# Sixteen gate tiles of the input projection, moved from the scan stage into the prompt attention

## What is computed

```python
h = rmsnorm(x, g_mix)
z = h @ w_in                    # 2048 x 8192: q | k | v | u | gate_a | gate_s
gate_a = sigmoid(z[..., U_END:U_END + D_MODEL])       # 16 column tiles of 128
gate_s = sigmoid(z[..., U_END + D_MODEL:])            # 16 column tiles of 128
q, k = partial_rope(rmsnorm(q, g_q), pos), partial_rope(rmsnorm(k, g_k), pos)
att = diff_attention(q, pos, segments, lam)   # (softmax1 - lam * softmax2) @ v, 8 heads, causal
branch_a = rmsnorm(att, g_head) * (1 - lam_init) @ w_attn_up
branch_s = glu(gelu(s5_scan(u, ...)) @ w_glu)
x = x + (gate_a * branch_a + gate_s * branch_s) @ w_out
# then an expert layer (peer_ffn) and an embedding layer, which the change does not touch
```

## Time and profile before

| what | us |
|---|---|
| median of 3 runs | 5486.42 (5477.35 to 5486.86) |
| the profiled execution | 5477.04 |
| its span | 5475.2 |
| PE busy | 4896.4 (89%) |
| PE weight loads busy | 4472.1 (82%) |
| POOL busy | 2502.2 (46%) |
| DVE busy | 2389.5 (44%) |
| ACT busy | 1624.6 (30%) |

### The profile page before, as it was taken

How to read it: one execution, slowest core, us unless ns; L and a number is a source line. 1 busy time by engine, 2 the same in 40 slices (tenths; PEclk the granted TensorE clock), 3 DMA queues, 4 the chain that set the end, 5 groups by cost and what they waited for, 6 DMA issues and landing times. The chain is left out here.

```text
span 5475.2 us, 82433 instructions
## 1 busy us (share of the span) xinstructions
PE 4896.4 (89%) x28806; PEld 4472.1 (82%) x28806; DVE 2389.5 (44%) x4202; ACT 1624.6 (30%) x2478; POOL 2502.2 (46%) x1751
## 2 busy tenths in 40 slices
PE   4899999745599598989979999999979999999979
PEld 3888899633333498979979999999979999999969
DVE  4366620126600422027747753444345666555521
ACT  2233322234300322232224533333333333333232
POOL 3377744100000143424483457777746665566433
PEclk6999999755599799999989999999989999999989
DMA  2222233112254244313234569999877777767423
GB/s 77 74 90 89 89 101 111 45 33 97 78 195 175 79 129 139 115 56 98 98 98 154 186 235 320 317 323 324 301 266 275 273 269 280 275 264 275 186 79 97
DMA packets 351200, 925.62 MB, mean 169 GB/s; under 512 B 41426, under 2 KB 118738, under 8 KB 300146
## 3 DMA queue, kind: packets, MB, share of 16 engines
q1 hardware_dynamic: 279090, 570.85, 31.2%
q0 software_dynamic: 37872, 272.25, 13.2%
q10 hardware_dynamic: 34128, 81.15, 4.0%
HBM read 838.10 MB, written 86.02 MB: 169 GB/s over the span
## 5 line engine op out<-in xcount | busy, mean ns | idle before, releaser
L2382 PE MATMUL val_y_ps<-val_wt,val_v 128*128 128x416 f32 x6144 | 1183.7, 353 | 29.9 <-POOL val_v L2367 29.9
L2382 PEld LDWEIGHTS val_y_ps<-val_wt,val_v 128*128 128x128 f32 x6144 | 1141.7, 188 | 72.0 <-issue 30.3
L239 PE MATMUL rt_acc<-xn_act,rt_w_hi 128*128 128x416 f32 x4096 | 1127.2, 356 | 33.2 <-POOL rt_w_rest L229 32.8
L229 POOL TENSOR_TENSOR rt_w_rest<-rt_w_raw,rt_w_hi 128x512 fp32r<-128x512 f32 x576 | 758.9, 1334 | 629.9 <-ACT rt_w_hi L224 625.6
L2367 POOL TENSOR_TENSOR val_v<-val_v_raw,val_v 128x2048 fp32r<-128x2048 f32 x128 | 591.8, 4623 | 464.9 <-ACT val_v L2413 464.9
L239 PEld LDWEIGHTS rt_acc<-xn_act,rt_w_hi 128*128 128x128 f32 x4096 | 762.8, 189 | 50.6 <-issue 23.5
L239 PE MATMUL rt_acc<-xn_act,rt_w_rest 128*128 128x416 f32 x2048 | 717.2, 350 | 0.0
L2463 DVE TENSOR_TENSOR out_xT<-out_xT,val_y_ps 128x416 f32<-128x416 f32 x512 | 300.1, 586 | 488.3 <-PE val_y_ps L2382 438.5
L224 ACT ACTIVATE rt_w_hi<-rt_w_raw 128x512 fp32r<-128x512 f32 x576 | 348.4, 629 | 512.8 <-DMA rt_w_raw<-in_peer_uT 302.9
L2289 DVE CUSTOM_DVE_ANT_0 rt_space<-rt_space,rt_mid 128x2048 f32<-128x2048 f32 x128 | 292.8, 2288 | 457.2 <-DMA rt_space<-in_peer_u,out_row_id 454.0
L239 PE MATMUL scan_acc<-in_act,scan_w_hi 128*128 128x272 f32 x2816 | 480.3, 293 | 3.3 <-POOL scan_w_rest L229 3.3
(11 more groups left out here) (393 smaller groups left out, 7500.7 us busy)
## 6 DMA issues: line engine op xcount, KB each, us to landing
rt_w_raw<-in_peer_uT SPq DMA_DIRECT2D x512, 256.0 KB
val_v_raw<-in_peer_vp SPq DMA_DIRECT2D x128, 1024.0 KB, 4.9
scan_w_raw<-in_w_in SPq DMA_DIRECT2D x224, 256.0 KB
pages_K<-in_cache_kT SPq DMA_DIRECT2D x64, 512.0 KB
pages_V<-in_cache_v SPq DMA_DIRECT2D x64, 512.0 KB, 7.1
hid_scratch<-rt_hid ACTq DMA_DIRECT2D x128, 208.0 KB
gate_scratch<-rt_space ACTq DMA_DIRECT2D x13, 2048.0 KB, 7.3
val_hid<-hid_scratch SPq DMA_DIRECT2D x32, 832.0 KB
```

Of the source, the lines that this page charges most:

```text
L229: e.tensor_tensor(self.rest[:, s, 0:nk, :], self.raw[:, s, 0:nk, :], self.hi[:, s, 0:nk, :].bitcast(F32), ALU.subtract).then_inc(self.rest ...
L239: mm = e.matmul(acc[:, h, 0:width], w[:, s, k, :], act[:, kt0 + k, a, col + h * width:col + (h + 1) * width], start=first and k == 0 and w ...
L2382: mm = e.matmul(y_ps[:, t % 2, 0:DW], v[:, c % 2, a, j, t * P:(t + 1) * P], wt[:, g % 2, j, b, :], start=j == 0 and a == 0 and b == 0, sto ...
```

## The change

- `N2` goes from 12 to 4: the second loop of the scan makes 8 gate tiles in place of 24.
- The other 16 gate tiles are made in the prompt attention, two for each head, in eight units. PE's program has a `gate_unit` call at eight places of `both`; ACT has `gate_hi` calls and two `gate_out` calls (evacuation and store); POOL, which had no program there, gets the remainders; SP gets eight unit loads a head. PE's program is written out for all eight heads, where it was a loop over pairs; the other engines keep the loop.
- The page loads leave the prompt attention. The sample attention loads all its pages itself, keys of sequence n + 1 ahead of the values of sequence n.
- PSUM for the gate tiles' accumulator comes from the values' transposes, which now go to the weights' buffer `tw` and a corner of `ss`. That adds waits: the turn of the values waits for the last copy of the weights of the head before, the first squares and the first turn of the weights for the copy of the values.
- The gates are stored without sigmoid. `stage_mix` applies it: after the fourth split of each tile ACT waits for both gates and takes their sigmoid in place; DVE waits for that.
- `k.act` stays in SBUF through the prompt attention, the attention's output takes the place of `k.uT`, and the page buffers are allocated only for the sample attention.

```diff
@@ stage_scan
-        N1, N2 = CT, 12
+        N1, N2 = CT, (KT - CT) // 2
-                e.activation(halves(zout[:, a, :]), src[:, :, 0:HALF],
-                             ACT.Sigmoid if sigmoid else ACT.Copy).then_inc(evac, 1)
+                e.activation(halves(zout[:, a, :]), src[:, :, 0:HALF], ACT.Copy).then_inc(evac, 1)
@@ stage_attention_prompt, SP
             def both(i, s):
                 load(i, s + 1, 0)
                 load(i, s + 1, 1)
-                load_pages(e, k, i * 2 + s)
+                gate_tiles(i, s, range(RING, RING + 2))
                 store_values(i, s)
                 load(i, s + 1, 2)
+                gate_tiles(i, s, range(RING + 2, RING + HEAD))
                 store_keys(i, s + 1)
@@ POOL
+            w.credit_rest(e)
+            with e.Fori(0, NH // 2) as i:
+                for u in range(PER):
+                    w.split_rest(e, i, PER, u)
@@ PE
+            def gate_unit(i, s, u):
+                if u % U == 0:
+                    e.wait_ge(acc_free, at(i, s, 2, u // U + 1))
+                w.multiply(e, i, PER, s * HEAD + u, acc, k.act, (u % U) * UNIT, u % U == 0, u % U == U - 1)
             def both(i, s, with_norm=True):
                 scores(i, s, 0)
                 turn_values(i, s)
+                gate_unit(i, s, 0)
                 if with_norm:
                     squares(i, s + 1, 0)
-                for b in range(4):
-                    ...
+                scores(i, s, 1)
+                gate_unit(i, s, 1)
+                if with_norm:
+                    rotate(i, s + 1, 0)
+                turn_weights(i, s, 0)
+                gate_unit(i, s, 2)
+                values(i, s, 0)
+                scores(i, s, 2)
+                if with_norm:
+                    squares(i, s + 1, 1)
+                gate_unit(i, s, 3)
+                turn_weights(i, s, 1)
+                values(i, s, 1)
+                scores(i, s, 3)
+                gate_unit(i, s, 4)
+                if with_norm:
+                    rotate(i, s + 1, 1)
+                turn_weights(i, s, 2)
+                gate_unit(i, s, 5)
+                values(i, s, 2)
+                gate_unit(i, s, 6)
+                turn_weights(i, s, 3)
+                gate_unit(i, s, 7)
+                values(i, s, 3)
-            heads(e, norm, both, lambda i, s: both(i, s, False))
+            heads(e, norm, both, lambda i, s: both(i, s, False), loop=False)
@@ ACT
+            def gate_out(i, s, t):
+                w.wait_used(e, i, PER, s * HEAD + (t + 1) * U)
+                e.wait_ge(z_stored[t], at(i, s, 16, 16))
+                e.activation(halves(zout[:, t, :]), acc[:, :, 0:HALF], ACT.Copy).then_inc(evac, 1)
+                e.wait_ge(evac, at(i, s, 2, t + 1))
+                e.sem_inc(acc_free, 1)
+                e.dma_start(k.z_dram[ds(i * 4 + (FIRST_GATE - CT + 2 * s + t), 1)].rearrange("o p n -> p (o n)"),
+                            zout[:, t, :]).then_inc(z_stored[t], 16)
             def both(i, s, with_norm=True):
                 if with_norm:
                     square(i, s + 1, 0)
                 copy_values(i, s)
+                gate_hi(i, s, 2)
+                exponents(i, s, 0)
+                if with_norm:
+                    deviation(i, s + 1, 0)
+                gate_hi(i, s, 3)
+                copy_weights(i, s, 0)
+                if with_norm:
+                    square(i, s + 1, 1)
+                gate_hi(i, s, 4)
+                exponents(i, s, 1)
+                gate_hi(i, s, 5)
+                copy_weights(i, s, 1)
+                gate_out(i, s, 0)
+                exponents(i, s, 2)
+                if with_norm:
+                    deviation(i, s + 1, 1)
+                gate_hi(i, s, 6)
+                copy_weights(i, s, 2)
+                gate_hi(i, s, 7)
+                exponents(i, s, 3)
+                if with_norm:
+                    gate_hi(i, s, 8)
+                copy_weights(i, s, 3)
+                if with_norm:
+                    gate_hi(i, s, 9)
                 e.wait_ge(pv_done, at(i, s, 4, 8))
                 e.activation(k.o[:, ds(i * 2 + s, 1), 0:NP].rearrange("p o n -> p (o n)"), o[:], ACT.Copy).then_inc(o_free, 1)
+                gate_out(i, s, 1)
@@ stage_attention_sample, SP
+            load_keys(e, k, 0)
+            for n in range(NB):
+                if n + 1 < NB:
+                    if n:
+                        e.wait_ge(s_done, n)
+                    load_keys(e, k, n + 1)
+                if n >= 2:
+                    e.wait_ge(pv_done, n - 1)
+                load_new(n)
+                load_values(e, k, n)
@@ stage_mix, ACT and DVE
+                        if u == 3:
+                            e.wait_ge(gate_in[a], i * 32 + 32)
+                            e.activation(gate[:, a], gate[:, a], ACT.Sigmoid).then_inc(gate_done, 1)
...
-                    e.wait_ge(gate_in[a], i * 32 + 32)
+                    e.wait_ge(gate_done, i * 2 + (a + 1))
```

More of the change, by code:

```diff
@@ L718, in _, with evacuate @@
             e.wait_ge(zero_done, 8)
-            def evacuate(i, t, second, sigmoid):
+            def evacuate(i, t, second):
                 a = t % 2
@@ L1071, in at, with heads @@
             return i * (2 * per) + (s * per + plus)
-        def heads(e, norm, both, last, chain=None, per=0):
+        def heads(e, norm, both, last, chain=None, per=0, loop=True):
             norm(0, 0)
+            if not loop:
+                for i in range(NH // 2):
+                    both(i, 0)
+                    (both if i < NH // 2 - 1 else last)(i, 1)
+                return
             with e.Fori(0, NH // 2 - 1) as i:
@@ L1116, in norm @@
             def norm(i, s):
-                for j in range(3):
+                for j in range(2):
                     load(i, s, j)
+                e.dma_start(raw[:, 2, :], k.z_dram[2 * NH]).then_inc(raw_in[2], 16)
+                gate_tiles(i, s, range(RING))
                 store_keys(i, s)
@@ L1196, in norm @@
                 for j in range(2):
-                    squares(i, s, j)
+                    squares(i, s, j, False)
                     rotate(i, s, j)
```

173 lines of the change are left out of this document (86 added, 87 removed).

## The result

The changed kernel takes 5344.72 us in the median of 4 runs (5340.08 to 5350.92), the kernel before 5486.15 us in the median of 4 (5477.35 to 5486.86): a ratio of 0.9746, 95% interval 0.9732 to 0.9761, or 141 us less. The forecast was 5372 us in a range of 5322 to 5425. The profiled executions lie closer together than the medians: spans of 5475.2 and 5343.9 us, 131.3 us less. The profiled one of before was 9 us under its median; where, is said further down.

A forecast was written before the change was run, and what follows sets the result against it. PE bounds the gate scan and sample attention, a dependency chain the prompt attention. Scan -193.0, heads +64.7, their start +1, pages +11.5, semaphores +1 sum to -114.8 us: 5372 us from the 5486.42 median, range 5322 to 5425.

The forecast's parts named there:

- part 1: Gate part of the scan: 16 tiles of 12.06 us leave, 193.0 us off; copy in place of sigmoid gains nothing.
- my layout: Prompt attention: timeline of one head in program order, PE at full clock, giving a pitch of 47.0 us for 40.0.
- No PE gap over 2.3 us: Prompt attention: no longer PE gap in a head, so the clock was taken as 2.4 GHz nearly throughout.
- G5, G6 and G7 on the path: End of an attention head: the last three of eight gate units unhidden; about 18 of 24.8 us fit.
- the first head's extra 2.3 us: First attention head, 42.3 us against 40.0: the extra would go because page loads no longer precede its values.
- POOL beside DVE: Prompt attention: GpSimd's subtractions make VectorE wait, taken as 0.5 us per head, bounds 0 to 2.
- The 8 us per head: Prompt attention: cost by the skill's exclusion rule if all ten two-input VectorE operations of a head met GpSimd.
- bounds of 10 to 25: Start of the sample attention: waiting for eight key pages costs +11.5 us, between 10 and 25.
- (1): Prompt attention: units hide almost fully, pitch 41, last head 33, stage +15, kernel 5322 us; chance 0.12.
- (2): Prompt attention: chain grows more than seen, pitch 53, last head 42, stage +108, kernel 5415 us; chance 0.18.
- (3): Prompt attention: PE's clock stays at 1.2 GHz, pitch 72, stage +264, kernel slower at 5571 us; chance 0.05.
- (4): Sample attention: keys and values come too late in every sequence, +20 us, kernel 5392 us; chance 0.05.

The follow-up runs named there:

- after_again: The changed kernel once more, unaltered, on the same chip as the combination of early exponents and key pages ahead: 5341.7 us, ratio 0.9742 to the kernel before.
- e1: The kernel before plus one ScalarE Gelu of one column ahead of the sample scan's loops: 5468.56 us against 5483.62, ratio 0.9963.
- e2: The kernel before with only the sigmoid moved: gates stored without it, the mixing stage applies it; 5464.88 us, ratio 0.9961.
- e11: The changed kernel with attention units of 12 matmuls for 24, first tile's weights reused, no later loads, splits or remainders: 5294.02 us.
- e6: The changed kernel with block 2's exponents and the next keys' square root ahead of the weights' copy and first evacuation on ScalarE: 5322.6 us, ratio 0.9704 to before.
- e3: The changed kernel without the 64 gate units in the prompt attention; order, waits and moved page loads stay: 5288.88 us.
- e5: The changed kernel with 2 matmuls per attention unit in place of 24; loads, splits, remainders and evacuations stay: 5329.28 us.
- e10: The changed kernel with 2 matmuls per attention unit in place of 24 and without GpSimd's remainders there: 5321.26 us.
- e4: The changed kernel with attention units reusing the first four units' weights, without own loads, splits and remainders; all matmuls and evacuations stay: 5325.13 us.
- e9: The changed kernel with the second sample sequence's keys issued only when the first's have landed: 5338.98 us.

## Why the prediction was right, and where it was off

**What bounds the kernel, and the scan.** Right: 16 tiles at 12.06 us gave -193.0, measured -192.9. Count times pitch holds to some tenths of a us where one engine bounds a stage at full clock. In other executions the clock drops once in the scan's second part, which then takes 2.5 us more (105.3 us at 0.97 in after_again, 102.8 at 1.00 in the changed kernel's profiled execution; 298.1 in e1, 295.6 before).

**The step that failed** is the sentence in part 1: "Copy in place of sigmoid there is off the path: no gain." In the scan itself it held. But the sigmoid also decided what the loops behind it start with, and with it the sample scan had 16 table loads of 1283 ns, 20.5 us of ACT in a loop that got 16.6 us shorter without them. e1 and e2 take them away with two different edits, and both shorten that loop by the same 16.6 us. That the diff changes nothing there was true of the stage's lines and not of its time. I read the three slow slices and laid out the attention, but never read by line the other stage in them, the sample scan: the 16 loads stood there. The median is missed by 27 us: the sample scan's 17.4 and the heads' 9.2, less the 5.1 that the start of the sample attention cost more; the rest is small terms and scatter. That errors of both signs partly cancel is luck. The Trainium skill says in "ScalarE activation tables: per-element evaluation and per-set limits", section "Table sets in the compiler and the runtime", that the back end places loads block by block for the longest run. The placing itself no run here shows. e1 shows that a loop's entry counts: its loop has the same instructions as the loop before and none of the loads.

**The heads.** Mechanism right, size 9 us too high (+64.7, measured +55.5). Set beside the head that began at 1176.64, my layout runs close: exponents of block 1 done at 18.0 (I had 17.4), of block 2 at 27.1 (26.4), second product at 33.5 (32.8), turn of block 2 at 35.1 (34.9), next head at 48.1 (47.0). But that is partly luck. This head has a third table load that my layout doesn't have; the next one, from 1224.74, is without it, and there the same points are at 16.3, 24.4, 31.0, 32.5 and 45.1. ScalarE ahead of the next head's square, in the one and in the other:

```profile
1178.94 1.28 ACT L1301 ACT_TABLE_LOAD   x1 [0.98 <-ACT att_zout L1293]
1180.23 0.66 ACT L1301 ACTIVATE att_sq<-att_raw 128x544 f32<-128x544 f32 x1
...
1226.74 0.66 ACT L1301 ACTIVATE att_sq<-att_raw 128x544 f32<-128x544 f32 x1 [0.68 <-ACT att_zout L1293]
```

The load stands at the top of each of the three trips of ACT's loop over pairs of heads, so in every kernel here, the one before too. In the first trip ACT is waiting anyway; in the other two it is on the path, and the first product of the norm ends at 12.9 in place of 11.2. These two heads take 48.0 us in the mean and the four others 45.3; in the kernel before it was 40.6 and 39.7. So the longer path of the changed kernel made a load dear that was nearly hidden, and that is some 0.6 of the 6.1 us; it wasn't taken away in any run.

The waits of PE were not what I had said either. TensorE and the others around the first product in the head that began at 1130.62, in the long one (1176.64) and in the short one (1224.74), columns as above:

```profile
1142.00:1150.00 8.00, 8.00 (x40) 6.77 (x41) 7.35 (x20) 4.16 (x9) 2.95 (x2) 0.79 0.14 36
...
1188.00:1196.00 8.00, 6.41 (x33) 5.87 (x35) 7.22 (x18) 4.16 (x9) 2.36 (x2) 0.79 0.20 47
...
1236.00:1244.00 8.00, 7.43 (x47) 6.12 (x48) 7.27 (x19) 4.17 (x9) 2.95 (x2) 1.00 0.12 35
```

Ahead of these products PE had waited 1.85, 2.53 and 1.84 us. "No PE gap over 2.3 us" was wrong by a little. But the wait alone doesn't decide the clock behind it: after 1.85 us it stood at 0.79, after 1.84 at 1.00. What the lower clock costs is the difference between two heads without the load, 46.0 and 45.1 us. Seven heads came to 324.9 us for my 332.5, the last to 35.9 (34.4 in after_again) for 37.5. That only part of 24.8 us fits the holes is right, but the split of the cost wasn't "G5, G6 and G7 on the path": e11 puts the first half of the matmuls at 0.4 us, and e6 gets 3.1 us from ACT's order. I had seen that order in the layout and counted it as a delay of block 2, not as a cost that could be had back.

One statement is wrong outright: that the first head's extra 2.3 us would go with the page loads. They are still there in e3, which loads no pages (42.3 us). In both kernels ACT's first square in that head waits for a raw tile, 11.05 us before and 10.81 after, whose load SP issues only behind the first store of keys; that this makes the 2.3 us is my reading, not tested.

**POOL beside DVE.** 0.5 us per head assumed; e5 and e10 give 0.8 without PE's load. DVE by line over the heads of the changed kernel (mean ns):

```profile
L1403 DVE TENSOR_TENSOR att_qk<-att_normed,all_const 128x544 f32<-128x544 f32 x14 | 15.6, 1113 | 0.0
L1407 DVE COPY heads_qk_sample<-att_qk 128x32 f32 (+1 forms) x14 | 9.7, 695 | 2.0 <-DVE att_qk L1406 1.5
```

The first was 720 ns, the second 181. Meetings fell on operations with slack, as said; the product of the norm kept its 785 ns. For products with two inputs in SBUF the trace agrees with the Trainium skill's rule in "SBUF — State Buffer", section "Who interferes with whom": with POOL idle (e4) the first line is back at 720, and the join of e5 goes from 977 to 541 in e10. The copy, which has one input and isn't of the kind that the prediction named, is back at 181 as well. Which operations are hit is a matter of timing: in e5, with POOL at work, these two have 720 and 181 too. The 8 us per head that I had worked out for all ten being hit did not come.

**The clock.** Right: 0.95 over the stage, though with short drops in most heads; e11 shows what the rise is worth. Whether transposes count as activity no run here isolates.

**Pages.** +16.6 for +11.5. The transfer was 14.4 us for 12.5, for a reason that e9 didn't find. And a term was left out: the stage now ends with an evacuation and its store, so from the last copy to DVE's first work behind it are 4.5 us, before 1.5. The bounds of 10 to 25 held. Keys and values never bound afterwards.

**Sample attention.** The +6.5 us that I had at 0 are, as far as the runs tell, scatter of the profiled execution of before. e1 and e2, which load the pages ahead as before does, have 289.5 and 291.2 us there, all other kernels 286.5 to 293.1; the 283.9 us of before is the odd one. With the 2.5 us by which its second part of the scan was shorter than theirs it makes up the 9 us under the median. What sets it in one execution wasn't found; in the changed kernel PE's clock stands at 0.60 to 0.66 in three stretches of 5 us there.

**Mixing.** Right: 318.2 us for 318.9, and e2 alone the same (317.9).

**The rivals.** (1) Nearly full hiding did not come at a pitch of 46.2, though its reason was half right: e6 gets to 43.0 with another order. (2) A pitch of 53 fell. (3) The low clock fell at 0.95; e3 and e11 show that the packing is what lifts it. (4) Pages in every sequence fell. The time of rival 1 is nearer to the result than mine, 5322 and 5372 to 5344.7, for a reason that neither had.

## What to carry to other kernels

Before removing an activation function, look at which table the next loops on ScalarE start with; loads that a loop repeats show as one line in the view by line, and a load at the top of a loop's body comes in every trip. Price work put into holes by every in-order queue it passes and by the clock that it brings: the first half here was nearly free and the second cost 4 us a head. Compare more than one execution before reading a difference of a us as a cost: one last head of 35.9 us was 34.4 in the same kernel's next trace. If the layout shows an engine idle ahead of an instruction whose successor is ready, change the order before paying for it.

## What the runs showed of the hardware that I had not expected

- A loop of copies and one Gelu had two table loads of 1283 ns in each of its 8 trips or none, by the function ahead of it (e1): 60.5 or 43.9 us for the loop.
- In the changed kernel a DVE copy of 32 columns took 181 ns, but 1.18 to 1.31 us in the 7 of 16 cases where it started just behind a 1.29 us subtraction of POOL; it then ended with it.
- A table load at the top of ACT's loop over pairs of heads made a head 0.9 us longer before and 2.7 us after.
- Behind the same waits of PE (0.47 and 1.52 us) the clock stood at 0.62 in one execution of the changed kernel and at 1.00 in another; the head took 35.9 and 34.4 us.
- Adding 96 matmuls of 272 columns to a 40 us head cost 0.4 us, at a granted clock of 0.83 in place of 0.56 (one execution of each).
